# Fourth-pass score masks, conditioning tiles and the last decay product moved within the order of steps

## What is computed

```python
for l in range(DEPTH):                                   # 2
    ada = (cond @ w_ada[l] + b_ada[l])[:, None, :]       # cond = silu(c), 6 x 2048 columns
    sh_m, sc_m, g_m, sh_f, sc_f, g_f = jnp.split(ada, N_ADA, axis=-1)
    h = x * (1.0 + sc_m) + sh_m
    y = hybrid_mixer(h, ...)       # h @ w_in -> retention, hgrn2, mamba2 -> concat @ w_out
    x = layer_norm(DEEPNORM_ALPHA * x + (1.0 + g_m) * y, ln_g[l, 0], ln_b[l, 0])
    h = x * (1.0 + sc_f) + sh_f
    y = jnp.square(jax.nn.relu(h @ w1[l])) @ w2[l]
    x = layer_norm(DEEPNORM_ALPHA * x + (1.0 + g_f) * y, ln_g[l, 1], ln_b[l, 1])
```

## Time and profile before

| | |
|---|---|
| median of 3 executions | 2477.61 us (2472.7 to 2478.1) |
| profiled execution | 2479.34 us, span 2477.5 us |
| PE busy | 2382.3 us (96% of the span) |
| DVE busy | 1897.4 us (77%) |
| ACT busy | 1161.7 us (47%) |
| POOL busy | 166.4 us (7%) |
| mean granted TensorE clock | 0.988 |
| DMA | 637.97 MB, mean 258 GB/s |

### The profile page before, as it was taken

One profiled execution on the slowest core, in us unless ns is written; L12 is line 12 of the kernel. 1 busy time (PEld: TensorE's weight loads), 2 busy tenths in 40 slices (PEclk: granted clock), 3 DMA queues, 4 the chain that ended last, 5 costly groups with the idle time before them and its releaser, 6 DMA issues.

```text
span 2477.5 us, 32067 instructions
## 1 busy us (share of the span) xinstructions
PE 2382.3 (96%) x12952; PEld 2056.7 (83%) x12952; DVE 1897.4 (77%) x2128; ACT 1161.7 (47%) x1505; POOL 166.4 (7%) x122
## 2 busy tenths in 40 slices
PE   3699999989999999999999999999999999999998
PEld 3689878869888888888889998888988888888886
DVE  6888988878989888888886578677888555655557
ACT  3354555546434435434445447554543443443442
POOL 0002100010011010020010110001001101101001
PEclk8799999999999999999999999999999999999999
DMA  9995678968898888888856446677778656656653
GB/s 372 407 372 205 201 266 298 372 214 304 334 354 319 308 320 305 317 312 312 319 187 181 137 127 220 228 272 263 274 274 291 189 188 194 187 188 194 186 190 119
DMA packets 179912, 637.97 MB, mean 258 GB/s; under 512 B 17260, under 2 KB 20020, under 8 KB 153780
## 3 DMA queue, kind: packets, MB, share of 16 engines
q1 hardware_dynamic: 174928, 617.94, 71.6%
q0 software_dynamic: 3296, 17.43, 1.8%
q10 hardware_dynamic: 1540, 0.55, 0.1%
HBM read 633.75 MB, written 2.10 MB: 257 GB/s over the span
## 4 chain that ended last, share of the span: by engine, by line
PE 85%; DVE 9%; DMA 3%; ACT 1%; issue 1%; ACTq 0%; DVEq 0%
PE PS L1681 42%; PE PS L1707 17%; PE PS L1709 9%; PE PS L1649 6%; PE PS L1690 4%; DMA FT<-in_w_ada 2%; DVE WL L1117 2%; PE PS L1663 2%; DVE FT L1348 1%; DMA MD<-in_m_d 1%; PE PS L1740 1%; DMA RAW<-in_w_out 1%; DVE FX L1058 1%; DVE CV L1323 1%; DVE FONE L1058 1%
## 5 line engine op out<-in xcount | busy, mean ns | idle before, releaser
L1117 DVE TENSOR_TENSOR WL<-RAW,WH 128x1024 fp32r<-128x1024 f32 (+1 forms) x800 | 994.5, 1255 | 473.2 <-ACT WH L736 471.4
L736 ACT ACTIVATE WH<-RAW 128x1024 fp32r<-128x1024 f32 (+1 forms) x800 | 831.9, 1045 | 1049.5 <-PE PS L1681 521.3
L1707 PE MATMUL PS<-HT,WH 128*128 128x512 f32 x1792 | 633.4, 399 | 0.0
L1709 PE MATMUL PS<-HT,WL 128*128 128x256 f32 x1792 | 503.1, 281 | 0.0
L1707 PEld LDWEIGHTS PS<-HT,WH 128*128 128x128 f32 x1792 | 336.7, 188 | 83.6
L1681 PE MATMUL PS<-WH,T2h 128*128 128x512 f32 x1208 | 373.9, 391 | 10.5 <-issue 7.6
L1681 PE MATMUL PS<-WL,T2h 128*128 128x512 f32 x1208 | 373.0, 390 | 0.0
L1681 PE MATMUL PS<-WH,T2l 128*128 128x512 f32 x1208 | 372.7, 390 | 0.0
L1709 PEld LDWEIGHTS PS<-HT,WL 128*128 128x128 f32 x1792 | 338.5, 189 | 0.2
L1681 PE MATMUL PS<-WH,HT 128*128 128x512 f32 x1024 | 288.0, 395 | 0.0
L1681 PEld LDWEIGHTS PS<-WH,T2h 128*128 128x128 f32 x1208 | 226.1, 188 | 57.9 <-issue 7.9
(11 more groups left out here) (295 smaller groups left out, 2140.5 us busy)
## 6 DMA issues: line engine op xcount, KB each, us to landing
RAW<-in_w SPq DMA_DIRECT2D x512, 512.0 KB, 4.2
RAW<-in_w_in SPq DMA_DIRECT2D x192, 512.0 KB, 4.0
FONE<-in_w_ada SPq DMA_DIRECT2D x77, 1024.0 KB, 6.6
FK<-in_w_ada SPq DMA_DIRECT2D x50, 1024.0 KB, 6.7
FT<-in_w_ada SPq DMA_DIRECT2D x32, 1024.0 KB, 10.4
RAW<-in_w_out SPq DMA_DIRECT2D x64, 512.0 KB, 5.9
FX<-in_w_ada SPq DMA_DIRECT2D x24, 1024.0 KB, 6.3
FH<-in_w_ada SPq DMA_DIRECT2D x9, 1024.0 KB, 11.7
```

What stands on the lines that cost most here:

```text
L736: act.activation(WH[:, wh_slot(layer, n), 0:w], RAW[:, k, 0:w], ACT.Copy).then_inc(hi_done.sem, 1)
L1117: tt(WL[:, k, 0:w], RAW[:, k, 0:w], WH[:, wh_slot(layer, n), 0:w].bitcast(F32), ALU.subtract).then_inc(lo_done.sem, 1)
L1707: mm(bank(p, j)[:, :], WH[:, wh, cols], HT[:, kt, :, :], start=kt == 0, stop=False, skip_group_check=True)
L1709: ins = mm(bank(p, j)[:, SEQ:2 * SEQ], WL[:, wl, cols], HTh[:, kt, :], start=False, stop=kt == KT - 1, skip_group_check=True)
```

## The change

Four edits, all in the order of work; no instruction is added or taken away.

```diff
             (0, [100, 101, 103, 106, 107, 109, 111, 112], range(32, 40)),
-            (0, [117, 118, 120, 121, 123, 124, 126, 130], range(40, 48)),
+            (0, [117, 119, 120, 121, 123, 124, 126, 130], range(40, 48)),
...
-        M_MUL, M_Y = [5, 6, 7, 8, 9, 10, 12, 13], [6, 7, 8, 9, 11, 12, 13, 14]
+        M_MUL, M_Y = [5, 6, 7, 8, 9, 10, 12, 13], [6, 7, 8, 9, 11, 12, 13, 15]
...
-                        if p in (2, 3) and kt in HG_M:
-                            hg_mask(layer, (p - 2) * 4 + HG_M.index(kt), p)
+                        if p == 2 and kt in HG_M:
+                            hg_mask(layer, HG_M.index(kt), p)
+                        if p == 3 and kt in HG_S:
+                            hg_mask(layer, 4 + HG_S.index(kt), p)
                         if (layer or n + AHEAD >= W_SLOTS) and n + AHEAD < FF0 * KT + 2:
                             lo_split(layer, n + AHEAD)
...
-                        for i in DOT_AT.get(layer * NUNIT + n, ()):
-                            dot(i)
                         if at in CONV:
...
                         if at == (8, 8):
                             row_stats(layer, x_add.at(layer, 4))
+                        for i in DOT_AT.get(layer * NUNIT + n, ()):
+                            dot(i)
```

## The result

The changed kernel took 2480.39 us (median of 20 executions, 2478.01 to 2483.62), the kernel before, timed beside it, 2477.27 us (20 executions, 2472.7 to 2479.52). The ratio is 1.0012, with a 95% interval of 1.0006 to 1.0017: 3 us slower, where 0.8 us faster was forecast.

A forecast was written before the change was run, and what follows sets the result against it. Vector's queue, with whatever blocks it, was taken to set the fourth pass's time while Tensor is nearly always busy. Pass 3 +5.8, less 3.65, 1.5 and 1.47, gave -0.8 us: 2476.8 us, own range 2473 to 2481, full range 2467 to 2483.

The forecast's parts named there:

- the walk: Layer 1's fourth pass, step by step: early masks make Vector wait for GpSimd, pass 4 starts 3.3 us later.
- Unknown: 0 to +1.7 each, I take 0: Pass 3: new falls of Tensor's clock would mostly land in the new waits; counted as 0.
- the room, 1.7 us: At (3, 15): a slowed score had 1.7 us before Vector was ready for the last mask.
- (5, 5): Layer 0: conditioning tile put last, so the MW wait and the clock fall behind it go; -3.65 us.
- (5, 12): Both layers: conditioning tile put last, so the MW waits of 0.76 us each go; -1.5 us.
- (7, 7): Conditioning tile no longer ahead of the T2 residuals: -1.47 us in layer 1, 0 in layer 0.
- SP's queue: Slot reloads and weight loads wait behind later tile products in (4, 6) and (7, 7); 0 to +2 us, taken 0.
- the last decay product: Moved from (5, 14) to (5, 15): Vector's later sum is covered by a unit, so 0; uncovered, 1.3 us per layer.
- The stated own range: 2473 to 2481 us around the forecast, for clock, SP's queue, layer 0's residuals and rounding.
- slower: the clock answers to the new waits: Rival, chance 0.17: every new pass 3 wait brings a 1.7 us clock fall reaching the path, +6.8; 2483.6 us.
- No lock: Rival, chance 0.21: blocking of (3, 4) not repeated or not holding the score, pass 3 about 4.4 us shorter per layer; 2468.

The follow-up runs named there:

- the filling: Idle matmuls ahead of the scores of (3, 9) and (3, 15), added to the changed kernel; 2477.92 us, ratio to before 0.9998.
- filled at (3, 15): Three idle matmuls ahead of the score of (3, 15) only, added to the changed kernel; 2480.15 us, ratio to before 1.0005.
- masks alone: Only the fourth pass's head masks moved one step earlier, against the kernel before; 2486.38 us, ratio 1.0036.
- changed again: The changed kernel rerun unaltered, on the chip of the single-place fillings, against the kernel before; 2481.24 us, ratio 1.0013.

## Why the prediction was wrong, point by point

- **Pass 3, the walk: right to about half a microsecond, up to its last line.** Layer 1, forecast beside the trace (0.56 us added for the shift): mask of (3, 6) at 1450.49, 1450.48; end of GpSimd's product 1457.7, 1457.63; score of (3, 9) from 1459.2, 1459.40; its mask 1461.4, 1461.68; next product 1468.6, 1468.84; mask of (3, 12) 1472.0, 1472.20; next product 1480.2, 1480.33; last mask 1484.1, 1484.64; pass 4 at 1485.5, **1487.01**. The blocking, its length, the evacuation behind Scalar's exponentials and both new waits came as written, the one at (3, 15) at 3.06 us for 3.4. Without clock falls the traces have +2.74 and +3.46 for +2.5 and +3.3.
- **The step that failed: "Unknown: 0 to +1.7 each, I take 0".** The term is the clock in the new waits of the fourth pass, which the sum put at nothing. It measured 2.26 us in layer 0 (46.06 - 43.80) and 1.47 in layer 1 (43.58 - 42.11), 3.7 together by these traces, and 3.5 by the ratios of the kernel with and without the filling. Both reasons for the 0 were wrong. At (3, 9) a fall can't hide in the wait, since it slows the score that comes behind it; the text said itself that there is no room there. At (3, 15) I counted the room, 1.7 us, on the way over the mask only. The fall lasts on through the unit between the score and pass 4: from the score's first matmul to pass 4 the changed kernel takes 6.62 us (1479.83 to 1486.45), the filled one 5.14, of which 1.07 is the wait for the mask. So 1.07 us of room stood against 2.55 of slowing, and in layer 0 against 1.5. The nearest row, the clock of 0.66 behind 2.03 us in the earlier trace rows, spoke for a value above 0 at waits of 2.3 to 3.5. The same trace had a counterexample as well: behind the wait of 2.09 us in the earlier trace rows the clock stayed up, at 1.00 in the next 5 us:

```profile
254.50:259.50 5.00, 5.00 (x43) 5.00 (x44) 4.86 (x10) 1.46 (x5) 0.00 (x0) 1.00 0.32 96
```

- **(5, 5), (5, 12): right.** The waits for MW are gone; pass 5 gained 4.63 in layer 0 (forecast 4.41) and 1.02 in layer 1 (0.76).
- **(7, 7): right in layer 1** (-1.76 for -1.47). In layer 0 the wait went too, and the stretch to (8, 0) is 0.58 us shorter, between the bounds, where I had taken 0. But that stretch varies by more than this from trace to trace, so a gain is not shown, and in the trace filled at (3, 15) 0.82 us of the wait are still there; the (8, 0) wait grew by 1.2 us as forecast.
- **SP's queue and the last decay product: 0**, as far as it shows. The kernels with and without that product and tile 119 have ratios of 0.9966 and 0.9967, with 3 us to either side. SP's queue was not tested by itself; the table's stretches add up to +1.9 us and the spans differ by 1.7, so nothing of the size of its +2 stands outside them.
- **The sum.** The forecast of -0.8, plus 3.7 for the clock, plus 0.4 for the walk, less 1.4 for the four gains that came out larger, is +1.9; the two traces show +1.7, the medians +3.1. The stated own range, 2473 to 2481, does not follow from its terms: they give 2475.3 to 2482.2. And of the old masks six, not seven, show the full 1.50 to 1.53 us; neither changes the sum.
- **The rivals.** What happened is "slower: the clock answers to the new waits", at 2480.4 instead of its 2483.6, as the falls at (3, 15) cost less than 1.7 and one at (3, 9) is not always there. "No lock" is refuted by the convolution rows. The Trainium skill's page "Advanced Engine Details and Errata", section "Mode Summary", names only Vector's two-port modes as what blocks and is blocked by GpSimd; read alone, as the prediction read it, it would have made that rival true, and the trace disagrees (3.37 for 1.51 us). The Trainium skill's page "SBUF — State Buffer", section "Who interferes with whom", says that an instruction with two SBUF inputs contends with a GpSimd instruction that reads SBUF, and the trace agrees: 3.37 us beside the product for the convolution, 1.28 for the mask's pair that has one input in PSUM, with or without the product beside it.

## What to carry to other kernels

When an instruction of Vector releases work on GpSimd, what matters is what Vector does in the next 2.5 us: here instructions with an input in PSUM went through untouched, and those with two inputs in SBUF waited for the whole product. So ask of a reordering not only whose wait ends earlier, but which instruction becomes the neighbour; putting the releasing instruction ahead of the mask instead of behind it was worth 12 us against the changed kernel, some 4 of them clock falls. It only regained what the early masks had lost: the old order without any of this was as fast.

A new wait on Tensor is to be charged its length and, from the nearest waits of the same length in the trace, a share of a clock fall; the fall is to be followed through all matmuls behind it, not only over the first dependence. Where a wait can't be avoided, a few idle matmuls in it cost nothing here, and a fall that they prevent had cost 0.4 to 1.6 us.

## What the runs showed of the hardware that was not expected

The same wait brings a fall in one execution and none in another: 2.31 us ahead of the score of (3, 9) in layer 1 gave 1.80 us in two traces (changed kernel, masks alone) and 3.26 to 3.28 in two others (changed again, filled at (3, 15)); 3.06 us at (3, 15) gave 1.83 in layer 1 of two traces and 2.2 to 3.4 elsewhere. All waits of 3.49 us, four, had a fall. Over pass 3 of all thirteen traces, by the granted clock of the 5 us behind each wait (1.00, or 0.50 to 0.69 with a fall):

| wait of Tensor, us | waits | with a fall |
|---|---|---|
| 1.37 to 1.78 | 8 | 0 |
| 2.02 to 2.17 | 11 | 7 |
| 2.31 | 4 | 2 |
| 3.05 and 3.06 | 8 | 6 |
| 3.49 | 4 | 4 |

In these waits length alone doesn't decide; what else does is open. It also means that one trace of a kernel holds 1.5 us of chance per such place, as much as most terms of the sum. The executions without a profile show the same scatter: of the kernel filled at both places, the six with a mean granted clock of 0.990 took 2477.2 us on average and the four with 0.988 took 2479.6. Of the kernel before, timed beside the repetition, fifteen had 0.988 and took 2477.5, fourteen had 0.987 and took 2479.2.

GpSimd's product takes 2.11 to 2.15 us when the mask follows EQ, 2.5 behind EQ and a narrow split, and 2.98 behind a wide split. Its record begins within 0.2 us of the split's, which takes 0.62 or 1.15 us, and it ends 2.0 to 2.1 us after the split. So the product waits for the one instruction of Vector that is under way, and then Vector waits for it.
